# State-space mixer: a head's decay exponents from one 128-row product and a small one, and scores masked once per group

## What is computed

```python
dt = jax.nn.softplus(dt_raw + dt_bias)
a = -jnp.exp(a_log).reshape(G, R)
cs = jnp.cumsum(dt_c * a, axis=2)                     # in each chunk
causal = jnp.tril(jnp.ones((L, L), dtype=bool))
seg = cs[:, :, :, None] - cs[:, :, None, :]
decay = jnp.exp(jnp.where(causal, seg, -jnp.inf))
cb = jnp.einsum('bclgn,bcsgn->bclsg', c_c, b_c)       # scores of a group
y_diag = jnp.einsum('bclsgr,bcsgrp->bclgrp', cb[..., None] * decay, x_dt)
...
y = (y_diag + y_off) + xs * d_skip
y = rmsnorm_per_group(y * silu(z)) * norm_w
return y @ w_out
```

## Time and profile before

| | |
|---|---|
| median of 3 runs | 1803.94 us (1803.49 to 1804.11) |
| profiled execution | 1803.99 us, of which the span is 1801.9 us |
| second mixer with its output | about 386 to 680 us in the span |
| a group's round with two heads | about 7 us |

### The profile page before, as it was taken

The page is one execution under the profiler, slowest core; times in us unless marked ns, Lnnn a source line. Parts: engine busy times, 40 slices in busy tenths (PEclk is TensorE's granted clock), DMA queues, the critical chain, the costliest instruction groups (busy, mean ns, idle before and its releaser), DMA issues.

```text
span 1801.9 us, 24943 instructions
## 1 busy us (share of the span) xinstructions
PE 1759.4 (98%) x8688; PEld 1093.9 (61%) x8688; DVE 1168.2 (65%) x1884; ACT 1130.7 (63%) x1582; POOL 1221.5 (68%) x1776
## 2 busy tenths in 40 slices
PE   7989999999999999999999999999999999999999
PEld 3546666655565556666666666666657776566665
DVE  6886777137988855777137857774267887577720
ACT  8887666455877667666464977665443544866641
POOL 7746777875545457777875658777864454577785
PEclk9999999999999999999999999999999999999999
DMA  7323444443233225444442024444532232244443
GB/s 266 105 94 129 152 141 146 161 152 122 75 90 94 94 84 175 152 141 147 160 135 96 25 71 140 146 148 146 158 120 80 75 94 71 93 154 150 142 158 121
DMA packets 64636, 225.38 MB, mean 125 GB/s; under 512 B 7808, under 2 KB 8192, under 8 KB 64128
## 3 DMA queue, kind: packets, MB, share of 16 engines
q1 hardware_dynamic: 63936, 221.79, 38.0%
q10 hardware_dynamic: 576, 2.01, 0.3%
HBM read 221.57 MB, written 2.10 MB: 124 GB/s over the span
## 4 chain that ended last, share of the span: by engine, by line
PE 77%; DVE 11%; ACT 6%; issue 4%; POOL 1%; DMA 0%; SPq 0%; DVEq 0%; ACTq 0%; POOLq 0%
PE psum L295 22%; PE psum L305 21%; PE psum L337 12%; PE psum L341 11%; PE psum L1778 3%; DVE psum L1586 2%; ACT psum L1455 1%; PE psum L2154 1%; ACT w_big L250 1%; PE psum L2189 1%; DVE psum L1671 1%; DVE arena L1574 1%; DVE arena L1633 1%; ACT L1488 1%; PE psum L2171 1%
## 5 line engine op out<-in xcount | busy, mean ns | idle before, releaser
L266 POOL TENSOR_TENSOR w_rest<-w_panel,w_big 128x256 bf16<-128x256 f32 x1660 | 1170.4, 742 | 531.3 <-ACT w_big L250 531.3
L295 PE MATMUL psum<-x_big,w_big 128*128 128x512 f32 x2248 | 658.4, 426 | 9.2 <-ACT x_big L387 7.0
L305 PE MATMUL psum<-x_rest,w_rest 128*128 128x512 bf16 x2248 | 556.0, 382 | 1.9 <-DVE x_rest L483 1.7
L250 ACT ACTIVATE w_big<-w_panel 128x1024 fp32r<-128x1024 f32 (+1 forms) x415 | 418.3, 1032 | 172.4 <-PE psum L341 99.5
L295 PEld LDWEIGHTS psum<-x_big,w_big 128*128 128x128 f32 x2248 | 418.5, 189 | 132.8 <-issue 25.9
L305 PEld LDWEIGHTS psum<-x_rest,w_rest 128*128 128x128 bf16 x2248 | 188.5, 98 | 283.2 <-issue 101.6
L701 DVE SCALAR_TENSOR_TENSOR psum<-ffn_raw,params,psum 128x512 f32<-128x512 f32 x352 | 264.6, 752 | 7.2 <-ACT psum L655 1.0
L693 DVE TENSOR_TENSOR ffn_raw<-psum,rstd 128x512 f32<-128x512 f32 x176 | 121.3, 691 | 141.3 <-PE psum L305 121.3
L655 ACT ACTIVATE psum<-ffn_raw,params 128x512 f32<-128x512 f32 x176 | 137.4, 782 | 101.9 <-DVE ffn_raw L693 101.6
L337 PE MATMUL psum<-g_big,w_big 128*128 128x512 f32 x704 | 199.3, 423 | 0.0
L547 DVE SCALAR_TENSOR_TENSOR x_resid<-psum,x_resid 128x512 f32<-128x512 f32 x64 | 43.8, 689 | 225.0 <-PE psum L341 217.0
(11 more groups left out here) (261 smaller groups left out, 1806.8 us busy)
## 6 DMA issues: line engine op xcount, KB each, us to landing
w_panel<-in_up SPq DMA_DIRECT2D x176, 512.0 KB, 3.3
w_panel<-in_dn SPq DMA_DIRECT2D x64, 448.0 KB, 3.1
w_panel<-in_ssd_in SPq DMA_DIRECT2D x41, 512.0 KB, 3.7
w_panel<-in_dn SPq DMA_DIRECT2D x32, 512.0 KB, 3.3
w_panel<-in_hgrn_in SPq DMA_DIRECT2D x32, 512.0 KB, 3.6
w_panel<-in_lru_in SPq DMA_DIRECT2D x18, 512.0 KB, 3.3
w_panel<-in_ssd_out SPq DMA_DIRECT2D x16, 512.0 KB, 3.5
w_panel<-in_swa_in SPq DMA_DIRECT2D x12, 512.0 KB, 3.6
```

The source lines that it names most:

```text
L250: act.activation(k.w1[:, slot, 0:words], k.w[:, slot, 0:words], ACT.Copy, scale=(SHIFT - 1) / SHIFT).then_inc(k.s("panel_big"), 1)
L266: rest = pool.tensor_tensor(k.w2[:, slot, a], k.w[:, slot, a], k.w1[:, slot, a].bitcast(F32), ALU.subtract)
L295: pe.matmul(out, k.w1[:, slot, q * m:(q + 1) * m], k.x1[:, q, :], start=q == 0, stop=False)
L305: mm = pe.matmul(out, k.w2[:, slot, q * m:(q + 1) * m], k.x2[:, q, :], start=False, stop=q == DT - 1)
```

## The change

`seg` issues two products instead of six. The left operand `head(g, r)` has 128 rows: 24 rows that pick the three parts of the head's sums, 12 rows that hold the head's own sums in each chunk (against minus ones in the right operand, so that they are subtracted), and 92 rows of a step table that adds -1e30 for later positions. The 92 rows bound 92 stretches of columns; 35 of these are two columns wide, and a second product with 35 rows and 4x35 columns (`odd_left`, `odd_right`) puts the missing -1e30 at their even columns. The scores are now masked once per group (`cb` on DVE, in place of ACT's copy), and `seg` on DVE takes the minimum of the exponential and 1.0 before it multiplies. The negated copy `ncs3` and its event `cs` are gone. Heads are ordered by head in group first, so that `heads_of` reads every fourth element. ACT loads six tables instead of two, partly into `k.y2`, which is free until the norm of a group; DVE waits for all of them (112 where it was 48) before L1549. SP moves the sums with twelve transfers of 8 rows and three of 4 rows.

```diff
-SSD_ROWS = 3 * SSD_DT
+SSD_ROWS = 3 * SSD_R
+SSD_BLOCK0 = SSD_ROWS + 3 * NC
+SSD_BLOCKS = P - SSD_BLOCK0
+SSD_DOUBLE = P - 1 - SSD_BLOCKS
...
     def seg(g, r):
...
-        pick = b.pick(g, r)
-        bank = 6 - r % 2
-        pe.matmul(k.ps[:, bank, :], pick, b.cs3[0:SSD_ROWS, :], start=True, stop=False)
-        for c in range(NC):
-            pe.matmul(k.ps[:, bank, chunk[c]], b.ncs3[0:SSD_ROWS, chunk[c]], pick, start=False, stop=False)
-        mm = pe.matmul(k.ps[:, bank, :], b.ident, b.mask.unsqueeze(1).to_broadcast([P, NC, P]), start=False, stop=True)
-        mm.then_inc(k.s("ssd_seg"), 1)
+        bank = k.ps[:, 6 - r % 2, :]
+        pe.matmul(bank, b.head(g, r), b.right[:, g, :], start=True, stop=False)
+        even = bank.rearrange("p (c l) -> p c l", l=P)[:, :, 0:2 * SSD_DOUBLE:2]
+        pe.matmul(even, b.odd_left, b.odd_right, start=False, stop=True).then_inc(k.s("ssd_seg"), 1)
...
 def ssd_sync(sp, k):
...
+    sp.wait_ge(k.s("mixer_landed"), 112)
     for part, ready in enumerate((3, 5, 6)):
         sp.wait_ge(k.s("ssd_chain"), ready)
         for c in range(NC):
-            sp.dma_start(b.cs3[SSD_DT * part:SSD_DT * (part + 1), c * P:(c + 1) * P], b.parts[part][rows]
+            sp.dma_start(right[SSD_R * part:SSD_R * (part + 1), c], b.parts[part][SSD_DT * c:SSD_DT * (c + 1)]
                          ).then_inc(k.s("ssd_cs_landed"), 16)
+        rows = slice(SSD_ROWS + NC * part, SSD_ROWS + NC * (part + 1))
+        sp.dma_start(b.left[rows], b.parts[part]).then_inc(k.s("ssd_cs_landed"), 16)
...
 def ssd_scalar(act, k):
...
     act.dma_start(b.table, k.dram["ssd_table"][:, 0:SSD_TABLE]).then_inc(k.s("mixer_landed"), 16)
+    for rows in (slice(0, SSD_ROWS), slice(SSD_BLOCK0, P)):
+        act.dma_start(b.left_words[rows], k.dram["ssd_tables"][rows, 0:SSD_LEFT]).then_inc(k.s("mixer_landed"), 16)
+    for rows, lo, to in ((slice(SSD_ROWS, P), 0, b.right), (slice(0, SSD_ROWS), S // 2, b.pairs)):
+        words = k.dram["ssd_tables"][rows, SSD_LEFT + lo:SSD_LEFT + lo + S // 2]
+        act.dma_start(to[rows].bitcast(F32), words.unsqueeze(1).to_broadcast([words.shape[0], SSD_G, S // 2])
+                      ).then_inc(k.s("mixer_landed"), 16)
...
-        act.wait_ge(k.s("ssd_cb_done"), g + 1)
-        act.activation(b.cb, k.ps[:, 4, :], ACT.Copy).then_inc(k.s("ssd_cb"), 1)
...
-            dve.wait_ge(k.s("mixer_landed"), 48)
+            dve.wait_ge(k.s("mixer_landed"), 112)
...
+    def cb(g, _):
+        dve.wait_ge(k.s("ssd_cb_done"), g + 1)
+        if g:
+            dve.wait_ge(k.s("ssd_m"), SSD_R * g)
+        dve.tensor_tensor(b.cb.rearrange("p (c l) -> p c l", l=P), k.ps[:, 4, :].rearrange("p (c l) -> p c l", l=P),
+                          b.causal.unsqueeze(1).to_broadcast([P, NC, P]), ALU.mult).then_inc(k.s("ssd_cb"), 1)
...
-        dve.tensor_tensor(b.m[:, r % 2, :], k.ps[:, 6 - r % 2, :], b.cb, ALU.mult).then_inc(k.s("ssd_m"), 1)
+        dve.scalar_tensor_tensor(b.m[:, r % 2, :], k.ps[:, 6 - r % 2, :], 1.0, b.cb, ALU.min, ALU.mult
+                                 ).then_inc(k.s("ssd_m"), 1)
```

More of the change, by code:

```diff
@@ L1098 @@
 SSD_DT = 32
-SSD_ROWS = 3 * SSD_DT
+SSD_ROWS = 3 * SSD_R
 SSD_SHIFTED = 9
-SSD_TABLE = 2 * P + SSD_DT * 65 // 2
+SSD_BLOCK0 = SSD_ROWS + 3 * NC
+SSD_BLOCKS = P - SSD_BLOCK0
+SSD_DOUBLE = P - 1 - SSD_BLOCKS
+SSD_BOUNDS = [2 * j for j in range(1, SSD_DOUBLE + 1)] + list(range(2 * SSD_DOUBLE + 1, P))
+SSD_LEFT = SSD_DT * P // 2
+SSD_TABLE = 2 * P + P // 2 + NC * SSD_DOUBLE // 2
 class SsdBuffers:
@@ L1114, in __init__ @@
         self.cs_t, self.dt_t, self.end_w, self.dec, self.dt_end = (a.take(NC, SSD_DT) for _ in range(5))
-        self.cs3 = a.take(S, dt=BF16)
         self.table = a.take(SSD_TABLE)
[L1117 to L1120, removed]
+        self.last_row, self.causal = self.table[:, 0:P], self.table[:, P:2 * P]
+        self.odd_left = self.table[0:SSD_DOUBLE, 2 * P:2 * P + P // 2].bitcast(BF16)
+        self.odd_right = self.table[0:SSD_DOUBLE, 2 * P + P // 2:SSD_TABLE].bitcast(BF16).rearrange("p (c n) -> p c n", c=NC)
+        self.left_words = a.take(SSD_LEFT)
+        self.left = self.left_words.bitcast(BF16)
+        self.right, self.pairs = k.y2[:, 0:SSD_T:SSD_TG, :], k.y2[0:SSD_ROWS, 1:SSD_T:SSD_TG, :]
         self.m, self.cb = a.take(2, S), a.take(S)
         self.ecs, self.off, self.b_t = a.take(384), a.take(384), a.take(384)
-        self.ncs3 = a.take(S, dt=BF16)
         self.ea = a.take(1)
@@ L1512, in early @@
             round_ahead(act, k, "ssd_out", len(used) - 1)
-    do = {"dt": dt, "cs": cs, "evict": evict, "decays": decays, "scores": scores, "seg": seg, "square": square, "root": root,
+    do = {"dt": dt, "evict": evict, "decays": decays, "scores": scores, "seg": seg, "square": square, "root": root,
           "normed": normed, "early": early, "silu": silu, "spread": spread, "round": round_}
@@ L1681, in ssd_vector @@
     do = {"dt": dt, "evict": evict, "taps": taps, "decays": decays, "turn": turn, "states": states,
-          "seg": seg, "post": post, "sum": sum_, "normed": normed, "rest": rest}
+          "cb": cb, "seg": seg, "post": post, "sum": sum_, "normed": normed, "rest": rest}
     for what, g, i in ssd_events():
@@ L1889, in hgrn_vector @@
     norm_vector(dve, k, 6)
-    dve.wait_ge(k.s("mixer_landed"), 80)
+    dve.wait_ge(k.s("mixer_landed"), 144)
     def half(h, i):
@@ L2513, in columns @@
     return np.ascontiguousarray(np.asarray(v).reshape(-1, P).T)
+SSD_HEADS = np.arange(SSD_DT).reshape(SSD_G, SSD_R).T.reshape(-1)
 def ssd_panels(w):
     x, B, C, dt = SSD_T * P, 2 * SSD_T * P, (2 * SSD_T + SSD_G) * P, (2 * SSD_T + 2 * SSD_G) * P
-    first = panels(w, DT, [span(dt, dt, dt, dt, width=SSD_DT)])
+    first = panels(w, DT, [np.tile(dt + SSD_HEADS, NC)])
     groups = []
@@ L2526, in ssd_panels, with ssd_tables @@
     return np.concatenate([first, panels(w, DT, groups)])
[L2529 to L2533, removed]
+def ssd_tables():
+    row, s, at, r = np.arange(P)[:, None], np.arange(P), np.arange(S), np.arange(SSD_R)
+    own = (row % SSD_R == r) & (row < SSD_ROWS)
+    bounds = np.zeros((P, 2))
+    bounds[SSD_BLOCK0:] = list(zip([0] + SSD_BOUNDS[:-1], SSD_BOUNDS))
+    later = np.where((row >= SSD_BLOCK0) & (s >= bounds[:, 1:]), -1e30, 0.0)
+    left = [own[:, n:n + 1] + later for n in r for _ in range(SSD_G)]
+    chunk = (row >= SSD_ROWS) & (row < SSD_BLOCK0) & ((row - SSD_ROWS) % NC == at // P)
+    block = (at % P >= bounds[:, :1]) & (at % P < bounds[:, 1:])
+    return bf16_words(np.concatenate(left + [block * 1.0 - chunk, np.repeat(own, 64, axis=1)], axis=1))
 def bf16_words(v):
@@ L2622, in layout @@
         np.tile((i == P - 1)[:, None], (1, P)).astype(np.float32),
-        bf16_words(np.eye(P)),
-        bf16_words(np.where(i[:, None] <= i, 0.0, -1e30)),
-        ssd_picks(),
+        (i[:, None] <= i).astype(np.float32),
+        bf16_words(np.where(i == 2 * i[:, None] + 1, -1e30, 0.0)),
+        bf16_words(np.tile(i[:, None] == np.arange(SSD_DOUBLE), (1, NC))),
         np.ones((P, P), np.float32),
     ], axis=1)
+    out["ssd_tables"] = ssd_tables()
     return out
```

31 lines of the change are left out of this document (12 added, 19 removed).

## The result

The median went from 1803.72 us (1802.58 to 1804.11) to 1812.32 us (1811.65 to 1813.63), a ratio of 1.0051 with the interval 1.0039 to 1.0063. The change makes the kernel slower by 8.6 us, or 0.5%, just beyond the upper end of the predicted range (1811.8). The profiled execution took 1813.63 us, with a span of 1811.8.

What follows compares the result with a forecast made beforehand. The DVE-ACT chain was taken to bound groups 0 to 2, PE only the last group. 1803.99 + 1.8 (scores) - 0.85 (last group) + 3.2 (tables) = 1808.1 us, range 1804.2 to 1811.8.

Steps and rivals of the forecast that it cites:

- I take 3.2 us: Before L1549: six tables, 1699 KB, land at 407.2 instead of the needed 404.0, delaying DVE 3.2 us, paid in full.
- the upper end of the term, 5.0: Tables' delay if the 736 KB transfer runs on four of sixteen engines: landing at 409.0, 5.0 us late.
- What bounds the kernel: Groups 0 to 2: the DVE-ACT chain, slightly longer than PE's work; only in the last group does it go through PE.
- The sign that the prediction named: PE waits before L1352 grow to about 1.4 us in a group's first round; not growing decides for PE as bound.
- speaking for the rival: Rival that PE was the bound after all: 10 to 12.5 us go, less 1.8 for scores, 1793 to 1796; 7%.
- the case of few engines: Rival: the 92-row transfer runs on a quarter of the engines, delay 5.0 or more, 1809.9 up to 1812 us; 27%.
- Two products for six: In `seg` on PE, a head saves 0.30 to 0.39 us, 10 to 12.5 over 32 heads; nothing in groups 0 to 2.
- 0.85 us of the last group: Group 3, chain through PE: 0.35 from the first round's second head plus 0.5 from three later rounds is given back.
- Masked scores: On DVE right ahead of the eviction: 0.60 us in each of three groups, 1.8 us; covered in group 3.
- The clamp, the strided factors, the negated copy: `seg` on DVE, reads in `heads_of`, a copy on ACT: 0 each; the clamp at most 3.8 us.
- ACT's and SP's queues: ACT issues four more transfers by 395.4, 0; SP's three more add 2.2 us to panel 10, still in time, 0.
- Clock: Rival: new waits before L1352 bring PE's clock down, about 1 us for each of three groups, 1811 us; 5%.

Runs made afterwards that it cites:

- own_pad_both: Changed kernel with a semaphore of their own for the four new tables, awaited by PE alone, and the 35-row and 24-row products zero-padded to 128 rows; 1803.09 us, ratio 1.0001.
- rows96: Changed kernel with the step table loaded in 96 rows (from row 32) instead of 92, 768 KB instead of 736; 1806.11 us, ratio 1.0015.
- rows16: Changed kernel with all tables loaded in row counts that divide by 16, 1923 KB in all instead of 1699; 1805.80 us, ratio 1.0012.
- own_wait: Changed kernel with the four new tables on a semaphore of their own, awaited only by PE at the first `seg`, not by SP or DVE; 1804.61 us, ratio 1.0009.

## Why the prediction was wrong

Its sign and its view of what bounds the kernel were right. The step that failed is one term, "I take 3.2 us" for the tables' delay. It was reckoned from the bytes at the rate of one 128-row transfer, and what set the delay was one 92-row transfer that kept 0.22 of 16 engines busy. The delay measured 9.4 us at L1550, 8.8 of it reached the first mark, and the upper end of the term, 5.0, was too low too. A second term was nearly all wrong, the 0.30 to 0.39 us that PE saves in a head, but it was rightly held off the path in groups 0 to 2 and cost the sum little.

- **What bounds the kernel.** Right. PE's waits behind the first heads grew in `own_pad_both` from 1.3 to 7.9 us while the period stayed, as the chain of waits had said and the busy share of 98% had not. The sign that the prediction named does not decide it: PE's waits before L1350 did not grow in the changed kernel (1.3 us, 1.4 before), which the prediction took as speaking for the rival, but here it is because PE saved next to nothing.
- **The tables.** The sum took a proportion from the 1280 KB row, one transfer of 128 rows, and left the case of few engines to a rival at 27%. `rows96` and `rows16` show that the rival was the right case. Its price was short as well. It counted 257 KB for each of the busiest engines at a panel's rate, and left out three panels that SP issued from 392.8 on: if they were spread evenly, they put 96 KB more on each engine. As an estimate, made afterwards, 353 KB at 32 KB in 1.8 us is 19.9 us, and with 392.7 + 1.8 the landing comes to 414.4, against 412.7 measured. No run without these panels was made. The transfers' view of that stretch shows the panels late in turn (9.1 us, where `rows96` has 5.2 and `rows16` 4.6):

```profile
w_panel<-in_ssd_in SPq DMA_DIRECT2D x3, 512.0 KB, 9.1
```

- **Two products for six.** The term of 0.30 to 0.39 us a head measured 0.03 (1.59 to 1.56 from head to head): neither the weight load of the 35-row product nor that of the product behind it was hidden. The term allowed up to 0.15 us from the second product to the next, where 0.22 passed, and nothing for the load ahead of it, where 0.32 passed for 0.23. The spread, with 24 rows for 96, stands 0.26 us ahead of the next product where it was 0.03, and gives up some 0.3 a round with the load ahead of it. Of the 0.85 us of the last group `own_wait` shows 0.15 (38.23 us from its last mark to the end of the stage, 38.38 before): the rounds are 4.62, not 4.5. In the changed kernel the clock's fall turned that into a loss of 1.4.
- **Masked scores.** Right: 0.60 us ahead of the eviction, 0.57 to 0.60 given back when moved. The period grew by only 0.43, so three groups cost 1.3 and not 1.8. The rest lies just ahead: the two decay products of the states (L1606, now L1607) take 0.90 and 1.06 us before and 1.10 and 0.69 after, 0.17 less together.
- **The clamp, the strided factors, the negated copy.** The clamp was right at 0: two L1641 take 1.29 us, as two L1633 took the earlier trace rows. The two L1607 are among the products that read the strided factors, so these did not slow them; whether the new order of the heads makes them 0.17 us faster, or something else, was not tried. One cast behind the scan (L1552, now L1553) takes 0.23 us where it took 0.72, which gives 0.5 of the tables' wait back. This is no gain of the change: it takes 0.23 in the four kernels whose DVE waits for the tables, and 0.72 again in `own_wait` and all that have the own semaphore.
- **ACT's and SP's queues.** Right at 0: six issues ended at 394.8. In `own_wait` the fifteen small transfers put SP's next panel off from 414.3 to 416.0, 1.7 us where 2.2 were forecast, and ACT rounds a panel at 420.9, where it did so at 421.1 before.
- **Clock.** It was tied to new waits before L1352, which did not come in the changed kernel. In `own_pad_both` they came, 7.9 us of them, and the clock stayed at 1.00. It fell in the long table wait instead, which cost nothing further, and in the last group.

The parts add up. Up to the first mark, 9.4 for the wait, less 0.5 for the cast and 1.1 for the fall at the turn that did not come, is 7.8, with 7.7 measured. Then come 1.3 up to the fourth mark and 1.4 in the last group, 10.4 in all. The stage starts 0.6 earlier, so 9.8 of the span's 9.9 are told.

What stays open: what decides whether the clock falls at the turn and in the last group, and what makes the two L1607 and the cast faster.

## What to carry to other kernels

Look at the first dimension of every new transfer before its bytes: here four rows more, 96 for 92, took 7.5 us off the wait, though they add bytes. Let each wait ask only for what its engine reads, since tables that PE needs some 30 us after they landed held up four engines here. And work taken from an engine that is 98% busy is no gain until the chain of waits goes through it; count its starts, not its instructions.

## What the hardware showed

- A 736 KB transfer of 92 rows kept 0.22 of the 16 engines busy at its end. With 96 rows the wait went from 9.4 to 1.9 us. Panels of 512 KB that SP issued in the same stretch were late too: 9.1 us from issue to landing beside the 92-row transfer, 5.2 beside that of 96 rows, 3.6 in the stage's median.
- A bf16 product of 140 columns whose left operand has 35 or 64 rows had its weights loaded only when it could start, and so had the product behind it: 0.54 us from L1331 to L295. With 65, 96 or 128 rows it was 0.25. This was seen behind a 128-row product of 512 columns, with rows counted from the first. The Trainium skill, TensorE: Matmul & The Clock Gate, "Step-by-step: what each phase is for", says that weight loads are pulled ahead of running products where row groups don't conflict or into the background buffer, and that the number of rows doesn't matter for the load's time. The trace agrees on the load itself (0.09 us with 35 rows, 0.10 with 128). Whether it was pulled ahead, though, changed with the number of rows in this case.
